# A hybrid attention layer on one Trainium2 core: the gated linear attention cut into pieces that stand between the units of the input projection

## The chip, the core and the metric

The kernel runs on one core of a Trainium2 chip. A core has five engines that run side by side and meet only at semaphores: TensorE (PE in the profile; its weight loads are listed as PEld), VectorE (DVE), ScalarE (ACT), GpSimd (POOL) and SyncE (SP), which here only issues DMAs. Work on data is done in SBUF, a memory of 128 partitions; TensorE writes to PSUM, eight banks of 128 partitions by 512 floats. The metric is the device time of one execution in microseconds (us); lower is better.

## What is computed

One layer over 1024 latent tokens and 256 context tokens of width 1024: a half-step SwiGLU FFN, then softmax attention and gated linear attention (GLA) from one input projection `w_in`, merged, and a second FFN. The part that the change touches, cut to its core:

```python
p_lat = split(n_lat @ w_in)      # q, k, v | gq, gk, gv, gz | low | gates   (also for the context)
attn  = block_attention(rope(norm(q)), rope(norm(k)), v)
# GLA, both directions, 4 heads, keys of 64, values of 128:
la = log_sigmoid(low @ w_decay + b_decay) / 16
b  = cumsum(la within a chunk)
o_inter = (gq * exp(b)) @ s                       # s: state at the chunk's edge
A[i, j] = sum_d gq[i,d] * gk[j,d] * exp(b[i,d] - b[j,d])      # j <= i
o = o_inter + A @ gv
s = exp(b_last) * s + (gk * exp(b_last - b)).T @ gv
gla = rms_norm(o) * g_gla * silu(gz)
y = sigmoid(gates_a + b_gate_a) * (attn @ w_branch[0]) + sigmoid(gates_b + b_gate_b) * (gla @ w_branch[1])
h = h + m_lat[5] * (y @ w_out)
```

## The kernel before, in words

Everything is kept with channels on the partitions and tokens along the free dimension. A weight block of 128 columns is a **panel**: SP loads it into `raw` (`load_panel`), DVE splits it into a high part `wh` and a low part `wl` (`split_panel`, L194 and L196), and TensorE multiplies in three passes, high by high, high by low, low by high (`three`, L219 to L221). Panels alternate between two slots; `panel_split` and `panel_used` count them.

The stage of the input projection (`win_*`) has 35 panels. A **unit** is one panel times one token chunk (512, 512 and, for nine of the panels, the 256 context tokens), 24 matmuls into one PSUM bank; the first two panels are done as a pair (6 units) while the norm of the FFN's result is still arriving, the other 73 units one after the other. Units go round all eight banks (`WIN_BANKS`), so TensorE may be eight units ahead of ACT, which evacuates each (`win_act`): k, v, gk, gv, low, q and gq stay in SBUF, gz (after Silu) and the sixteen gate panels (after Sigmoid with their bias) go through the four buffers `staged` to `gate_dram`.

Only when all units are done comes the GLA, in four steps written one behind the other on each engine:

- `gla_state_*`: values turned (L1225), decay logits (L1232), their log-sigmoid on ACT (L1267 to L1273, three table switches), 40 scans on DVE (L1306), decayed keys (L1315), then for 18 chunk steps the keys turned (L1240), copied by ACT (L1284), multiplied with the values (L1254) and added to the state by DVE (L1338, L1340).
- `gla_intra_*`: for each half of the latent tokens eight score levels. POOL forms the differences of `cum` (L1428 to L1431), ACT exponentiates them (L1405), DVE multiplies them into `qc` and `kc` (L1463, L1465), TensorE forms the scores (L1373), DVE takes the part that a mask selects (L1482). After eight levels TensorE applies scores to values and queries to states (L1385, L1388).
- `gla_out_*`: squares (ACT L1512), their sums (PE L1530), Ln and Exp (ACT L1519, L1523), then scaling, gating and the split into `glah` and `glal` on DVE (L1537 to L1544).
- `qk_*`: squares of k and q (ACT L1579), their sums (PE L1609), root, reciprocal, rotary embedding, and after that the softmax attention `att_*` and the merge.

Of the kernel before, what the change touches and what calls it, by code (L numbers as in the profile page):

```python
# [100 lines left out]
def build(nc, x, c, ctx_in, c_ctx, w_mod, b_mod, g_norm, w_ffn_up, w_ffn_down, w_in, g_q, g_k,  # L101
# [64 lines left out]
    part_loaded, gate0_loaded, select_loaded = rows_loaded[0:4], rows_loaded[4:8], rows_loaded[8]  # L166
    cols_ready = sem("cols_ready")
# [31 lines left out]
    def pn(p):  # L199
        return (p // 2, p % 2)  # L200
# [774 lines left out]
    gk_f, gv_f = at("gk_f", 0, [2, TOK]), at("gv_f", 10, [4, TOK])  # L975
    k_f, v_f = at("k_f", 30, [TOK]), at("v_f", 35, [TOK])
    q_f = at("q_f", 120, [4, SEQ])
    gq_f, low_f = at("gq_f", 193, [2, SEQ]), at("low_f", 201, [TOK])
    staged = at("staged", 164, [4, 512])

    la = at("la", 40, [4, TOK])
    kk = la
    cum = at("cum", 60, [4, TOK])
    vtok = at("vtok", 80, [N_CHUNKS, GLA_HEADS * DV])
    states = at("states", 100, [2, 9, 2, DV])
    wdec = at("wdec", 148, [512])
    ktok = at("ktok", 150, [2, 256])
    last = at("last", 152, [4, N_CHUNKS])
    elast = at("elast", 152.5, [4, N_CHUNKS])
    dexp = at("dexp", 154, [2, TOK])  # L990
    gla_o = at("gla_o", 10, [GLA_HEADS, SEQ])
    eq, ek = at("eq", 140, [2, 512]), at("ek", 144, [2, 512])
    qc, kc = at("qc", 148, [2, 512]), at("kc", 152, [2, 512])
    eqs, eks = [eq, at("eq_b", 48, [2, 512])], [ek, at("ek_b", 52, [2, 512])]
    qcs, kcs = [qc, at("qc_b", 164, [2, 512])], [kc, at("kc_b", 168, [2, 512])]
    scores = at("scores", 156, [2, 4, 2, P])
    qdec = at("qdec", 40, [2, 2, 512])
    gz_s = at("gz_s", 80, [GLA_HEADS, SEQ])
    gla_r = at("gla_r", 140, [8, 512])
    gla_n = at("gla_n", 201, [2, 512])  # L1000
    glah, glal = at("glah", 40, [GLA_HEADS, SEQ], F32R), at("glal", 56, [GLA_HEADS, SEQ], F32R)

# [85 lines left out]
    def ffn0_last_dve(dve):  # L1090
# [7 lines left out]
        for q in range(24):  # L1098
# [5 lines left out]
            if q == 20:  # L1104
                split_panel(dve, pn(win_p0))
# [1130 lines left out]
```

## Time and profile before

| | us |
|---|---|
| median of 3 runs | 3028.68 (3025.79 to 3031.61) |
| the profiled execution | 3022.72, span 3020.9 |
| PE busy in it | 2803.9 (93%) |
| DVE, ACT, POOL busy | 1502.4, 556.7, 508.0 |
| mean granted clock of TensorE | 0.953 of full |

The page cuts the span in 40 slices of 75.5 us. Each digit is the busy share of a slice in tenths, and PEclk is the clock that was granted to TensorE, in tenths of full speed (2.4 GHz; 5 is 1.2 GHz). The lines of engines show where the kernel leaves its dense pattern: slices 19 to 24 of the line of PE and of the clock.

```profile
PE   8999999999999999999456869998999999999998
...
PEclk9999999999999999999666679999999999999999
```

### The profile page before, as it was taken

The page shows a single profiled execution, that of the slowest core. Times are in us where ns is not written, and L with a number is a line of the kernel's source. Part 1 is how long each engine was busy: PE and PEld are TensorE (multiplying, and loading weights), DVE is VectorE, ACT ScalarE, POOL GpSimd, SP SyncE. Part 2 cuts the span into 40 slices and gives each one's busy share as a digit, 9 for nine tenths or more (in the row PEclk, how much of TensorE's full clock was granted, in tenths as well). Part 3 has the DMA queues.
Part 4 walks back from the last instruction along what each step waited for, and adds up shares of the span by engine and source line. Part 5 has one row for each costly group of instructions (what it writes and reads, how often), then busy time and mean ns, then how long its engine had stood idle before and what let it go on. Part 6 is the DMA issues. An engine that isn't in the chain of part 4 may idle for free. (4 is left out here: it accounts for less than half of the span.)

```text
span 3020.9 us, 35198 instructions
## 1 busy us (share of the span) xinstructions
PE 2803.9 (93%) x14298; PEld 2292.2 (76%) x14298; DVE 1502.4 (50%) x2336; ACT 556.7 (18%) x1039; POOL 508.0 (17%) x400
## 2 busy tenths in 40 slices
PE   8999999999999999999456869998999999999998
PEld 3888888888888788887255647776777888888887
DVE  7544445444434611111776488885645444444444
ACT  4100000000000411112422447773011000000002
POOL 0065655554200000000063001211000000000001
PEclk9999999999999999999666679999999999999999
DMA  7112122222111211332000100002421111111111
GB/s 271 46 60 70 60 68 89 84 84 94 54 35 42 84 37 43 94 98 75 0 1 1 42 1 1 1 1 91 156 68 35 49 49 44 49 46 49 49 49 70
DMA packets 192127, 176.65 MB, mean 58 GB/s; under 512 B 6989, under 2 KB 148602, under 8 KB 191994
## 3 DMA queue, kind: packets, MB, share of 16 engines
q1 hardware_dynamic: 186016, 164.22, 17.1%
q10 hardware_dynamic: 5978, 10.56, 0.9%
q8 instruction: 95, 1.56, 0.2%
q14 instruction: 38, 0.31, 0.0%
HBM read 155.89 MB, written 18.87 MB: 58 GB/s over the span
## 5 line engine op out<-in xcount | busy, mean ns | idle before, releaser
L219 PE MATMUL psum<-nh,wh 128*128 128x512 f32 (+2 forms) x1688 | 612.9, 363 | 1.4 <-DVE wl L196 1.4
L220 PE MATMUL psum<-nl,wh 128*128 128x512 f32 (+2 forms) x1688 | 612.2, 363 | 0.0
L221 PE MATMUL psum<-nh,wl 128*128 128x512 f32 (+2 forms) x1688 | 611.8, 362 | 0.0
L194 DVE CAST wh<-raw 128x1024 fp32r<-128x1024 f32 x175 | 125.8, 719 | 695.0 <-PE psum L221 689.4
L219 PEld LDWEIGHTS psum<-nh,wh 128*128 128x128 f32 (+1 forms) x1688 | 316.7, 188 | 53.8 <-DVE wl L196 1.8
L221 PEld LDWEIGHTS psum<-nh,wl 128*128 128x128 f32 (+1 forms) x1688 | 316.5, 188 | 51.4
L220 PEld LDWEIGHTS psum<-nl,wh 128*128 128x128 f32 (+1 forms) x1688 | 316.7, 188 | 50.6
L844 DVE SCALAR_TENSOR_TENSOR h<-psum,gates,h 128x512 f32<-128x512 f32 (+1 forms) x400 | 270.8, 695 | 150.9 <-PE psum L221 149.1
L219 PE MATMUL psum<-hidh,wh 128*128 128x512 f32 (+1 forms) x880 | 329.2, 374 | 11.3 <-DVE hidl L828 7.6
L812 ACT ACTIVATE silu_a<-psum 128x512 f32<-128x512 f32 (+1 forms) x110 | 61.2, 556 | 1488.1 <-PE psum L221 1488.1
L220 PE MATMUL psum<-hidl,wh 128*128 128x512 f32 (+1 forms) x880 | 324.8, 369 | 0.0
L221 PE MATMUL psum<-hidh,wl 128*128 128x512 f32 (+1 forms) x880 | 324.1, 368 | 0.0
L219 PE MATMUL psum<-n1h,wh 128*128 128x512 f32 x704 | 274.3, 390 | 0.5 <-DVE wl L196 0.5
L221 PE MATMUL psum<-n1h,wl 128*128 128x512 f32 x704 | 273.9, 389 | 0.0
L220 PE MATMUL psum<-n1l,wh 128*128 128x512 f32 x704 | 273.9, 389 | 0.0
L196 DVE TENSOR_TENSOR wl<-raw,wh 128x1024 fp32r<-128x1024 f32 x175 | 226.7, 1295 | 6.1
L823 DVE TENSOR_TENSOR prod<-silu_a,psum 128x512 f32<-128x512 f32 (+1 forms) x110 | 69.7, 634 | 303.2 <-PE psum L221 300.4
L219 PEld LDWEIGHTS psum<-hidh,wh 128*128 128x128 f32 x880 | 165.8, 188 | 47.6 <-issue 13.7
L221 PEld LDWEIGHTS psum<-hidh,wl 128*128 128x128 f32 x880 | 165.6, 188 | 28.5
L220 PEld LDWEIGHTS psum<-hidl,wh 128*128 128x128 f32 x880 | 166.0, 189 | 26.9
L927 POOL TENSOR_TENSOR y_rows<-y_scaled,g_row 128x1024 f32<-128x1024 f32 x4 | 9.5, 2377 | 922.9 <-ACT y_scaled L921 922.9
L219 PEld LDWEIGHTS psum<-n1h,wh 128*128 128x128 f32 x704 | 132.2, 188 | 28.6 <-DVE wl L196 0.9
(251 smaller groups left out, 3866.7 us busy)
## 6 DMA issues: line engine op xcount, KB each, us to landing
raw<-in_w_ffn_up_dram SPq DMA_DIRECT2D x88, 512.0 KB, 3.9
mod_part<-in_w_mod_dram SPq DMA_DIRECT2D x96, 256.0 KB, 4.2
raw<-in_w_ffn_down_dram SPq DMA_DIRECT2D x44, 512.0 KB, 3.4
raw<-in_w_in_dram SPq DMA_DIRECT2D x34, 512.0 KB, 3.8
mod_raw<-in_w_mod_dram SPq DMA_DIRECT2D x12, 1024.0 KB, 13.7
gates_saved<-staged ACTq DMA_DIRECT2D x40, 256.0 KB, 2.0
merge_gate<-gates_saved SPq DMA_DIRECT2D x8, 1024.0 KB, 5.0
x_rows<-in_x_dram SPq DMA_DIRECT2D x8, 512.0 KB, 7.8
```

Source lines behind the costliest of these rows:

```text
L194: nc.vector.tensor_copy(wh[:, par, 0:n], raw[:, par, 0:n]).then_inc(panel_split, 1)
L196: nc.vector.tensor_tensor(wl[:, par, 0:n], raw[:, par, 0:n], wh[:, par, 0:n].bitcast(F32), ALU.subtract).then_inc(panel_split, 1)
L219: pe.matmul(o, hi_w, hi_x, start=first, stop=False)
L220: pe.matmul(o, hi_w, lo_x, start=False, stop=False)
L221: return pe.matmul(o, lo_w, hi_x, start=False, stop=last)
L812: nc.scalar.activation(silu_a[:, c, 0:w], ps[c][:, 0:w], ACT.Silu).then_inc(self.a_free, 1)
L823: nc.vector.tensor_tensor(prod[:, c % 2, 0:w], silu_a[:, c, 0:w], ps[3 + c][:, 0:w], ALU.mult).then_inc(self.b_free, 1)
L844: nc.vector.scalar_tensor_tensor(hk, down, gates[:, self.gate_i, k, s:s + 1], hk, ALU.mult, ALU.add).then_inc(self.down_free, 1)
L927: nc.gpsimd.tensor_tensor(y_rows[:, i, :], y_scaled[:, i, :], g_row[:, :], ALU.mult).then_inc(y_gained, 1)
```

## The change

The GLA is no longer a stage of its own. Each of its pieces is tied to the number of a unit (`LOGIT_UNITS`, `SCAN_UNITS`, `VTURN_UNITS`, `BATCH_UNITS`, `ITEM_UNITS`, `OUT_UNITS` and others), and `win_pe`, `win_act` and `win_dve` call `decay_*`, `state_*` and `intra_*` behind every unit:

- The panels are reordered: low, gk, k, v, gv, gq, gz, q, gates. k, v and q are copied to `kvq_dram` through `staged` and loaded back at the end (`weave_end_sp`); the gates are stored as they are, and the sigmoid is done in the merge, on ACT.
- The units behind the pair use two PSUM banks in turn (`RING_BANKS`) in place of eight; the other six serve the GLA.
- The state steps run in 12 batches of up to 4 chunks, one head pair and direction at a time, behind units 32 to 48. The intra part is 32 **items**, four groups (head pair times half of the tokens) of eight levels, each half as wide as a level before (128x512 in place of 128x1024). They stand behind units 49 to 73, five items to every four units, so seven units have two. Behind units 55, 62, 68 and 74 stands the output of a group, behind the next unit its sums of squares.
- A group's result is stored to `gla_dram` and the whole loaded back as `gla_n`; its high part is made by ACT, its low part by POOL, in `qk_act` and `gla_low_pool`; DVE did both.

```diff
-    WIN_BANKS = (4, 6, 7, 5, 0, 3, 1, 2)
+    PAIR_BANKS = (4, 6, 7, 5, 0, 3)
+    RING_BANKS = (1, 2)
...
     def win_pe(pe, panel0, norm):
...
-            if u >= 8:
-                pe.wait_ge(win_evac, u - 7)
+            if u >= PAIR_UNITS + 2:
+                pe.wait_ge(win_evac, u - 1)
             for k in range(KT):
                 mm = unit_k(u, k)
             done(u, mm)
+            decay_pe(pe, u)
+            state_pe(pe, u)
+            intra_pe(pe, u)
...
     def win_dve(dve, panel0):
-        for i, (_, width, _, _) in enumerate(win):
-            if i >= 2:
-                split_panel(dve, pn(panel0 + i), KT * width)
+        dve.wait_ge(h_saved, 16)
+        nc.vector.memset(wdec[0:2 * RANK, :], 0.0).then_inc(dec_zero, 1)
+        split_panel(dve, pn(panel0 + 2), KT * win[2][1])
+        for u in range(PAIR_UNITS, N_UNITS):
+            i, c = win_units[u]
+            if c == 0 and i + 1 < len(win):
+                split_panel(dve, pn(panel0 + i + 1), KT * win[i + 1][1])
+            decay_dve(dve, u)
+            state_dve(dve, u)
+            intra_dve(dve, u)
...
+    LOGIT_UNITS = [6, 7, 8, 9, 10, 11, 35, 36, 37, 38, 39, 40]
+    LN_UNITS, SCAN_UNITS = [8, 11, 37, 40], [10, 13, 39, 42]
+    BATCH_UNITS = [32, 33, 34, 35, 36, 37, 42, 43, 44, 45, 46, 47]
+    ITEM_UNITS = [49 + 4 * n // 5 for n in range(N_ITEMS)]
+    OUT_UNITS = [ITEM_UNITS[N_SCORES * g + N_SCORES - 1] + 1 for g in range(N_GROUPS)]
...
+    def intra_act(act, u):
...
+        if u - 1 in OUT_UNITS:
+            g = OUT_UNITS.index(u - 1)
...
+            for par in range(2):
+                act.wait_ge(o_ss, 2 * g + par + 1)
+                nc.scalar.activation(gla_r[par][:, :], ps[OUT_PAIR[par]][:, :], ACT.Ln, bias=eps, scale=1.0 / DV)\
+                    .then_inc(o_ln, 1)
+            for par in range(2):
+                act.wait_ge(o_ln, 2 * g + par + 1)
+                nc.scalar.activation(gla_r[par][:, :], gla_r[par][:, :], ACT.Exp, scale=-0.5).then_inc(o_rs, 1)
...
+    def weave_end_sp(sp):
+        sp.wait_ge(g_oz, N_GROUPS)
+        wait_saved(sp, len(staged_units))
+        sp.dma_start(k_f[:, :], kvq_dram[0]).then_inc(kvq_loaded, 16)
+        sp.dma_start(q_f[:, :, :], kvq_dram[2:6, :, 0:SEQ].rearrange("n p t -> p n t")).then_inc(kvq_loaded, 16)
+        sp.dma_start(v_f[:, :], kvq_dram[1]).then_inc(kvq_loaded, 16)
+        sp.dma_start(rope_t[:, :, :], rope.rearrange("a p t -> p a t")).then_inc(rope_loaded, 16)
+        sp.wait_ge(panel_used, merge_p0)
+        sp.wait_ge(g_stored, 32 + 16 * N_GROUPS)
+        sp.dma_start(gla_n[:, :, :], gla_dram).then_inc(gla_back, 16)
...
     def qk_act(act):
...
+        act.wait_ge(kvq_loaded, 80)
         for u in range(len(qk_units)):
             square(u)
+        act.wait_ge(gla_back, 48)
+        for hd in range(GLA_HEADS):
+            nc.scalar.activation(glah[:, hd, :], gla_n[:, hd, :], ACT.Copy).then_inc(o_hi, 1)
...
     def merge_act(act):
+        for n in range(KT):
+            act.wait_ge(gate_loaded[n % 2], 16 * (n // 2 + 2))
+            for b in range(2):
+                a = A_BGATE + KT * b + n
+                g = merge_gate[:, n % 2, b, :]
+                nc.scalar.activation(g, g, ACT.Sigmoid, bias=cols_a[:, a:a + 1]).then_inc(m_gate, 1)
...
-            dve.wait_ge(gate_loaded[n % 2], 16 * (n // 2 + 2))
+            dve.wait_ge(m_gate, 2 * n + 2)
```

How the rows stand on TensorE. Before, behind the last three matmuls of the last unit (`nh`, `nl` are the normed input, `wh`, `wl` the panel) comes the whole state step:

```order
L219 MATMUL psum<-nh_50,wh 128x512
L220 MATMUL psum<-nl_51,wh 128x512
L221 MATMUL psum<-nh_50,wl 128x512
L1225 MATMUL psum<-cst,gv_f 128x128 x40
L1232 MATMUL psum<-low_f,wdec 128x512 x2
L1232 MATMUL psum<-low_f,wdec 128x256
```

Now, around unit 56 (lines are one higher in the changed file: L220 to L222 is `three`), with the end of the output of group 0 (L1457, L1459) and item 8 (L1482, `gk_f`) ahead of it, and the sums of squares (L1467) and item 9 behind it:

```order
L1457 MATMUL psum<-scores,vlat_119 128x128
L1459 MATMUL psum<-qdec,states 128x128 x2
L1482 MATMUL psum<-eq_123,gk_f 128x128 x8
L220 MATMUL psum<-nh_50,wh 128x512
L221 MATMUL psum<-nl_51,wh 128x512
L222 MATMUL psum<-nh_50,wl 128x512
...
L1467 MATMUL psum<-cum,cst 128x512 x2
L1482 MATMUL psum<-eq_124,ek_126 128x128 x8
```

What was one run of GLA matmuls behind the last unit is now groups of 2 to 24 matmuls between units.

On ACT, the end of the GLA before (`sq` and `gla_r` belong to the norm of the outputs):

```order
L1405 ACTIVATE ek_b<-ek_b 128x1024
L1512 ACTIVATE sq<-gla_o 128x512 x2
L1519 ACT_TABLE_LOAD
L1519 ACTIVATE gla_r<-psum,cols_b 128x512
...
L1523 ACT_TABLE_LOAD
L1523 ACTIVATE gla_r<-gla_r 128x2048 x2
```

Now, behind unit 56, between the evacuation of that unit (L1202, and L1205, its store) and the exponentials of items 10 and 11 (L1518):

```order
L1202 ACTIVATE staged<-psum 128x512
L1205 DMA gates_saved<-staged 128x512
L1500 ACT_TABLE_LOAD
L1500 ACTIVATE gla_r_132<-psum,cols_b 128x512
L1500 ACTIVATE gla_r_133<-psum,cols_b 128x512
L1504 ACT_TABLE_LOAD
L1504 ACTIVATE gla_r_132<-gla_r_132 128x512
L1504 ACTIVATE gla_r_133<-gla_r_133 128x512
L1518 ACTIVATE eq_123<-eq_123 128x512
L1518 ACTIVATE ek_125<-ek_125 128x512
```

The norm of a group, with its two table loads, now stands ahead of the exponentials of the next items, once per group.

On SP, the end of the stage before, from the last panels of `w_in` to the first of the merge:

```order
L205 DMA raw<-in_w_in_dram 128x8x128 x26
L1202 DMA cst<-in_shape_consts_dram 128x1152
L1205 DMA wdec<-in_w_decay_dram 16x256
L1206 DMA wdec<-in_w_decay_dram 16x256
L1504 DMA gz_s<-gates_saved 128x4x1024
L1572 DMA rope_t<-in_rope_tables_dram 128x2x1024
L205 DMA raw<-in_w_branch_dram 128x8x128
```

and now:

```order
L206 DMA raw<-in_w_in_dram 128x8x128
L1619 DMA gla_saved<-gla_f 128x2x512
L1625 DMA k_f<-kvq_saved 128x1280
L1626 DMA q_f<-kvq_saved 128x4x1024
L1627 DMA v_f<-kvq_saved 128x1280
L1628 DMA rope_t<-in_rope_tables_dram 128x2x1024
L1631 DMA gla_n<-gla_saved 128x4096
L206 DMA raw<-in_w_branch_dram 128x8x128
```

Three loads (k, q, v) now stand at the point where the attention begins, and `gla_n` behind the rotary table.

## Rows read from the trace of the kernel before

**Rows 1.** Stretches: length, busy of PE, PEld, DVE, ACT, POOL, clock, DMA share, GB/s

```profile
1046.00:1425.20 379.20, 378.42 (x1749) 312.23 (x1748) 58.91 (x63) 47.67 (x75) 0.00 (x0) 1.00 0.24 71
1425.20:1512.00 86.80, 39.67 (x218) 21.15 (x218) 57.54 (x124) 37.52 (x54) 0.00 (x0) 0.67 0.01 4
1512.00:1602.00 90.00, 59.86 (x376) 49.95 (x374) 56.96 (x68) 16.68 (x18) 46.55 (x36) 0.60 0.00 1
1602.00:1684.00 82.00, 55.51 (x358) 46.35 (x356) 50.17 (x56) 16.26 (x17) 26.86 (x20) 0.65 0.02 5
```

**Rows 2.** Chain that ended last, in order of time: start, us, what

```profile
1702.07 18.09 PE psum L1609 x84
1724.79 6.33 PE psum L1631 x28
```

**Rows 3.** Timeline of PE in the linear attention: start, us from first to last end

```profile
1431.63 1.98 PE L1232 MATMUL psum<-low_f,wdec 32*128 32x512 f32 x4
...
1497.48 0.67 PE L1254 MATMUL psum<-vtok,ktok 128*64 128x128 f32 x8 [0.38 <-DVE states L1340]
1498.08 0.44 PE L1240 MATMUL psum<-cst,la 128*128 128x128 f32 x2
...
1575.23 0.79 PE L1385 MATMUL psum<-scores,vtok 128*128 128x128 f32 x2
...
1577.11 0.79 PE L1385 MATMUL psum<-scores,vtok 128*128 128x128 f32 x2
...
1616.82 2.06 PE L1373 MATMUL psum<-qc,kc 64*128 64x128 f32 x32 [2.52 <-DVE kc L1465]
1623.22 3.79 PE L1373 MATMUL psum<-qc_b,kc_b 64*128 64x128 f32 x32 [4.35 <-DVE kc_b L1465]
...
1651.62 0.49 PE L1385 MATMUL psum<-scores,vtok 128*128 128x128 f32 x2 [2.85 <-DVE scores L1482]
...
1652.83 0.80 PE L1385 MATMUL psum<-scores,vtok 128*128 128x128 f32 x2
...
1691.02 2.22 PE L1530 MATMUL psum<-sq,cst 128*128 128x512 f32 x4 [0.23 <-ACT sq L1512]
```

**Rows 4.** Lines of DVE: duration ns min/median/max, first and last start

```profile
L1306 DVE TENSOR_TENSOR_SCAN cum<-cst,la x40: 395/397/424, 1459.8 to 1476.7; 128x128 f32<-128x128 f32 x40
...
L1465 DVE TENSOR_TENSOR kc_b<-gk_f,ek_b x8: 1206/2054/2056, 1529.2 to 1645.5; 128x1024 f32<-128x1024 f32 x8
...
L1482 DVE COPY_PREDICATED scores<-cst,psum x56: 694/718/761, 1537.5 to 1650.9; 128x512 f32<-128x512 int32 x56
```

**Rows 5.** Timeline of ACT around a table switch

```profile
1449.01 0.47 ACT L1267 ACTIVATE la<-psum,cols_b 128x256 f32<-128x256 f32 x1 [0.39 <-PE psum L1232]
1449.50 1.28 ACT L1270 ACT_TABLE_LOAD   x1
1450.79 1.27 ACT L1270 ACTIVATE la<-la 128x1280 f32<-128x1280 f32 x1
```

**Rows 6.** Groups by line and shape: busy us, mean ns, idle before

```profile
L1512 ACT ACTIVATE sq<-gla_o 128x512 f32<-128x512 f32 x8 | 4.9, 620 | 40.6 <-DVE gla_o L1447 40.6
...
L1519 ACT ACTIVATE gla_r<-psum,cols_b 128x512 f32<-128x512 f32 x8 | 5.5, 685 | 2.0 <-PE psum L1530 1.8
```

**Rows 7.** DMA issues: out<-in, count, KB each, median us from issue to landing

```profile
gates_saved<-staged ACTq DMA_DIRECT2D x40, 256.0 KB, 2.0
merge_gate<-gates_saved SPq DMA_DIRECT2D x8, 1024.0 KB, 5.0
...
gz_s<-gates_saved SPq DMA_DIRECT2D x1, 2048.0 KB, 8.0
...
rope_t<-in_rope_tables_dram SPq DMA_DIRECT2D x1, 1024.0 KB, 10.1
```

**Rows 8.** A stretch of 4 us, columns as in rows 1

```profile
1576.00:1580.00 4.00, 4.00 (x14) 3.10 (x14) 0.00 (x0) 0.00 (x0) 2.32 (x3) 0.50 0.00 0
```

**Rows 9.** Timeline of DVE: its first instruction on a gate in the merge

```profile
2088.82 0.69 DVE L2043 TENSOR_TENSOR ma<-psum,merge_gate 128x512 f32<-128x512 f32 x1 [1.24 <-PE psum L221]
```

More of the change, by code:

```diff
@@ L976, in build @@
+    glah, glal = at("glah", 40, [GLA_HEADS, SEQ], F32R), at("glal", 56, [GLA_HEADS, SEQ], F32R)
+    gla_n = at("gla_n", 56, [GLA_HEADS, SEQ])
     k_f, v_f = at("k_f", 30, [TOK]), at("v_f", 35, [TOK])
     q_f = at("q_f", 120, [4, SEQ])
[L978 to L985, printed above, removed]
@@ L1048, in build, with wait_saved @@
+    def wait_saved(eng, n):
+        for b in range(4):
+            eng.wait_ge(saved[b], 16 * len(range(b, n, 4)))
     win_done, win_evac = sem("win_done"), sem("win_evac")
@@ L1269, in gla_state_act @@
             act.wait_ge(g_abs, 3 * (j + 1))
-            nc.scalar.activation(la[:, j, :], la[:, j, :], ACT.Exp, scale=-1.0).then_inc(g_exp, 1)
-        for j in range(4):
+            nc.scalar.activation(a, a, ACT.Exp, scale=-1.0).then_inc(g_exp, 1)
             act.wait_ge(g_exp, j + 1)
-            nc.scalar.activation(la[:, j, :], la[:, j, :], ACT.Ln, bias=1.0).then_inc(g_ln, 1)
-        act.wait_ge(g_last, 4)
-        nc.scalar.activation(elast[:, :, :], last[:, :, :], ACT.Exp, scale=1.0 / GATE_NORM).then_inc(g_elast, 1)
@@ L1276, in gla_state_act @@
[L1276 to L1288 removed]
+            nc.scalar.activation(a, a, ACT.Ln, bias=1.0).then_inc(g_ln, 1)
@@ new lines, in intra_pe @@
+        for n in range(N_ITEMS):
+            if ITEM_UNITS[n] != u:
+                continue
+            g, lv, t, tok = item(n)
+            pe.wait_ge(g_qk, 2 * n + 2)
+            if n >= 2:
+                pe.wait_ge(g_pred, 2 * (n - 1))
+            else:
+                pe.wait_ge(g_state, N_STATES)
+            for cc in range(4):
+                for par in range(2):
+                    r = slice(DK * par, DK * par + DK)
+                    here = slice(cc * P, (cc + 1) * P)
+                    w = gk_f[r, t, tok][:, here] if lv == 0 else eks[n % 2][r, here]
+                    mm = pe.matmul(ps[SCORE_BANKS[n % 2][par]][:, here], w, eqs[n % 2][r, here],
+                                   start=True, stop=True)
+            mm.then_inc(g_sc, 1)
@@ L1545, in gla_out_dve, with gla_low_pool @@
+    def gla_low_pool(pool):
+        for hd in range(GLA_HEADS):
+            pool.wait_ge(o_hi, hd + 1)
+            nc.gpsimd.tensor_tensor(glal[:, hd, :], gla_n[:, hd, :], glah[:, hd, :].bitcast(F32), ALU.subtract)\
                 .then_inc(o_lo, 1)
```

701 lines of the change are left out of this document (364 added, 337 removed).

## The prediction

> **What bounds the kernel now.** I read the page first: PE is busy in 93% of the span, and only slices 19 to 24 of its line fall below 9, together with the granted clock. Then I cut the span at the stage borders. [rows 1]: in the input projection PE is busy for 378.4 of 379.2 us at full clock, while DVE, ACT and POOL have 59, 48 and 0 us of work. In the linear attention (GLA) that follows, PE is busy for 155 of 259 us, and at a mean clock of 0.60 to 0.67, so for most of it at 1.2 GHz and not 2.4. The stage starts at 1425.20, and the first sum of the softmax attention's norm starts at 1702.07 [rows 2]. So 276.9 us are spent, with PE waiting for other engines or running slow, right behind a stage in which the other engines are nearly empty. DVE paces the intra part: between two score levels PE waits for `kc` for 2.5 to 4.4 us [rows 3].
>
> **Term 1, what leaves: -276.9 us**, the whole stretch.
>
> **Term 2, what PE gets between the units.** Each piece still costs PE its own time, now at full clock if the clock holds. The instructions are as many as before (an f32 matmul is two instructions in the trace). From [rows 3], starts read against starts:
> - 32 items of 16 instructions: at full clock 32 instructions take 2.06 us, so 1.03 each, 33.0.
> - 32 output groups (one L1385, two L1388, six instructions). At half clock one takes 1577.11 - 1575.23 = 1.88, so 0.94 is the floor; with the clock falling it took 1652.83 - 1651.62 = 1.21. I take 1.0: 32.
> - 18 chunk steps of L1254: 1498.08 - 1497.48 = 0.60, 10.8.
> - 76 transposes: a pair shows 0.44 with its drain, a stream of eight instructions 0.67, so between 0.08 and 0.22 each; I take 0.15, as most stand in groups of four and eight: 11.4.
> - 24 instructions of L1232: 1.98 for four of 512 columns, 16 x 0.50 + 8 x 0.25 = 10.
> - 16 of L1530: 2.22 / 4 = 0.55, 8.8.
>
> Together +106 (floor 98, ceiling 118).
>
> **Term 3, waits in the woven stage.** 73 units make 378.4 us [rows 1]; 7 of them are of half size, so a full unit is 378.4 / 69.5 = 5.44 us. What must fit under it:
> - The ring of two banks (in place of eight): unit u waits for the evacuation of u-2, so ACT has a whole unit of slack. The log-sigmoid puts two table loads and two activations of 1280 columns (2 x 1.28 + 2 x 1.27 = 5.1 us, [rows 5]) behind one unit, which fits; the ten scans of 0.40 [rows 4] with three wide DVE instructions around them exceed a unit, but their taker stands two units on. I put 0 on this part.
> - Items: DVE must take the last item (two L1482, 1.44 us), split a panel in every other unit, and form two products of half the old width, 0.6 us each alone and 1.03 while POOL works (half of 1206 and of 2054 ns, [rows 4]). Some 3.5 to 5.5 us under 5.44 + 1.03: no wait in units with one item; in the seven with two, I expect about 1 us each: 8.
> - Behind an output, ACT must do the norm before the next exponentials. With E the end of unit 56: evacuation and store to E+1.0, table to 2.3, two Ln of 0.69 [rows 6] to 3.7, table to 4.9, two Exp (as the squares, 0.62) to 6.2, exponentials of item 10 to 7.4, its products to 8.6 or 9.5. PE, with sums 2.2 and item 9 1.0, ends unit 57 at E+8.7. So 0 to 0.8 us here and about as much for item 11; three such places, 4.
>
> Together +12. Below 0 is excluded, since a wait can only add. The ceiling is what a level waits now, (2.5 + 4.4) / 2 [rows 3], at half width 1.7, on 28 items: 48.
>
> [rows 5] also shows that the engine goes on at once at both ends of a table load: the activation before ends at 1449.48, the load runs from 1449.50, the next starts at 1450.79. The Trainium skill (ScalarE: Activation LUTs, What ACT_TABLE_LOAD costs) counts about 2.66 us for every switch of sets, the load and a drain of 1.38. By that rule each of the three norms would come 2.8 us later, and the sum would be 8 us higher; the trace disagrees, and the sum goes by the trace.
>
> **Term 4, the clock.** The units keep PE dense, so I expect 2.4 GHz in nearly all of the stage. But the output groups are a doubt: in 1576 to 1580 PE is busy for all of 4.00 us, and the clock is 0.50 [rows 8], and it had stayed so since the output began. So a run of eight groups can by itself be too thin for full clock. Half clock on all four outputs would cost 32 x 0.88 = 28; on the items too, (3.79 - 2.06) / 2 each [rows 3], 28 more. Nearest in kind is the dense stage around them; I take +8 (0 to 35).
>
> The Trainium skill (TensorE: Matmul & The Clock Gate, Why this matters for your kernels) advises to keep TensorE busy to hold the fast clock and puts the fall down to idle gaps. By it alone this term would be 0, and the sum 8 us lower; the row of a busy engine at 0.50 does not agree with busy time as the whole condition.
>
> **Term 5, the end of the stage.** The last unit is evacuated (0.6), stored (2.0 to landing, [rows 7]), and only then are k, q and v loaded, 3328 KB, for all of which ACT waits before its first square. The nearest row: 2048 KB of gz and 1024 KB of the rotary table queued behind it landed within 10.1 us, so 3328 KB need 10.9. With the issues and the first square (0.62, [rows 6]) it is +14.5 (12 to 18). PE has nothing then, and the norm that follows runs slow, as it does now.
>
> **Term 6, behind it.** `gla_n` (2048 KB) and the rotary table follow the three loads, some 10 us, under the 18.1 us of L1609 [rows 2]. ACT casts 4 x 1024 columns (about 1.05 each, 4.2 us) between its last square and the root; it has some 1.5 us to spare there, so the root comes 2.7 later, and with it the reciprocal, the v split and L1631. DVE's old tail (`gla_n`, `glah`, `glal`) ran beside L1609, so its going gives nothing. In the merge 16 sigmoids stand on an idle ACT; gates take 5.0 us to land [rows 7], a table load and two activations make 3.4 more, and DVE's first use at 2088.82 waits for PE [rows 9], so 0 to 2, I take 1. Together +3.7.
>
> **The sum:** 3022.7 - 276.9 + 106 + 12 + 8 + 14.5 + 3.7 = 2890, against the profiled execution. The median of the runs is 6 us (0.2%) above that execution; I give **2892**.
>
> **Rivals.**
> - *The items are paced by POOL, ACT and DVE, not by PE* (the ceiling of term 3): +36, 2928. For it: the chain differences, exponential, product, score is in series, and DVE's products double in time under POOL. Against it: an item may use a whole unit of 5.44 us, and POOL starts on it an item early. Chance 0.15.
> - *Half clock at outputs and items:* 56 in place of 8, 2940. Chance 0.11.
> - *Shorter than forecast:* no waits, full clock throughout, transposes at their floor: 2862 to 2872. Chance 0.09.
> - *Slower than before:* the f32 matmuls between the units pull the clock of the whole stage down to what they had alone, 0.63. Then 378 + 106 us of column-bound work become 768, which is +284: 3176. The point from which it decides: 135 us of gain are gone when the mean clock of the stage is below 484 / 619 = 0.78. Against it: more than three quarters of the work are the dense units that have 1.00 now. Chance 0.03.
> - *It isn't woven after all:* the rows of the order show GLA matmuls between the units, so only waits could undo it. Within the first rival.
>
> The forecast, 2872 to 2915, has 0.62. The range 2862 to 2938 leaves out about 0.15. A measurement of this kernel tells about 0.2% (6 us) from no change. Faster 0.96, same 0.01, slower 0.03: all cases but one lie 85 us or more below.
>
> **What the profile after would show.** The stage from the first unit behind the pair to the last should last 485 to 520 us with PE busy over 95% and clock over 0.95; L1482 16 instructions in about 1.0 us; the L1457/L1459 run in 8 us, 15 if the clock falls; PE idle before L1482 released by DVE `ek`, about 12 us in all, most in units with two items and behind a norm; a gap of about 15 us ahead of the sums of the qk norm, released by ACT's squares, these by the DMA of q or v; the root some 3 us later after it. I am wrong if idle before L1482 exceeds 40 us, if the clock in the stage is under 0.9, or if the DMA gap is over 20 us.

## The result, and the profile after

| | before | after |
|---|---|---|
| median | 3028.19 (3025.79 to 3031.61) | 2880.62 (2879.48 to 2885.50) |
| profiled execution | 3022.72, span 3020.9 | 2880.92, span 2879.0 |
| PE busy in it | 2803.9 (93%) | 2753.7 (96%) |
| mean granted clock | 0.953 | 0.983 |

The ratio is 0.9515, 95% interval 0.9498 to 0.9531. Beside the last experiments the kernel after ran again, with a median of 2884.27 and a ratio of 0.9528 (0.9513 to 0.9542); so two series of the same kernel differ by 0.13%.

The lines of PE and of the clock over the span of the kernel after, in 40 slices of 72.0 us. Before, five slices in a row stood at 4, 5, 6, 8 and 6; of this hole two slices are left, at 7 and 5:

```profile
PE   8999999999999999999997599979999999999998
...
PEclk9999999999999999999997799999999999999999
```

The woven stage and the gap behind it, in the columns of [rows 1]: length, busy of PE, PEld, DVE, ACT, POOL, clock, DMA share, GB/s.

```profile
1047.35:1543.80 496.45, 492.60 (x2711) 393.17 (x2712) 235.74 (x360) 151.02 (x240) 84.44 (x112) 1.00 0.23 69
1543.80:1559.40 15.60, 1.44 (x7) 0.88 (x6) 0.00 (x0) 1.35 (x3) 0.00 (x0) 0.71 0.71 281
```

The same units had 59 us of DVE work beside them before; now they have 236, and PE is still busy 99% of the time at full clock. Between the units and the first sum of the attention's norm lay 276.9 us [rows 1, 2]; now it is 14.2.

The longest waits of PE in the kernel after (what waited, for what, us in total, times, longest):

```profile
PE psum L1863 <- DVE ptl L1965: 28.2, 63, 1.8
PE psum L1701 <- ACT qk_sq L1666: 14.2, 1, 14.2
...
PE psum L1482 <- DVE ek L1593: 3.7, 3, 1.9
```

L1482 is now the score item. It waits 3.7 us in all, where a level waited 2.5 to 4.4 us each time [rows 3]. The new 14.2 us are the wait for k, q and v. PE in the woven stage (start, us from first to last end, count, idle time and releaser): a single item with the first matmul of the unit behind it, and the first output group of a run.

```profile
1376.98 1.16 PE L1482 MATMUL psum<-eq,ek 64*128 64x128 f32 x16 [0.74 <-DVE ek L1593]
1378.08 0.50 PE L220 MATMUL psum<-nh,wh 128*128 128x512 f32 x1
...
1404.83 0.38 PE L1457 MATMUL psum<-scores,vlat 128*128 128x128 f32 x2
...
1405.78 0.49 PE L1457 MATMUL psum<-scores,vlat 128*128 128x128 f32 x2
...
1406.84 0.49 PE L1457 MATMUL psum<-scores,vlat 128*128 128x128 f32 x2
```

The item is 16 instructions, the next unit begins 1.10 us after it began. An output group takes 1405.78 - 1404.83 = 0.95 for the first and 1406.84 - 1405.78 = 1.06 for those that follow, at full clock; it took 1.88 in [rows 3].

### The profile page after: what moved, and what is told of

It reads as the page before. It is cut to its first block, busy times and chain, and to the rows that moved or that the text cites. A ratio compares the mean times of both kernels' runs of the same rounds, so it can differ in the third digit from the quotient of the medians.

```text
span 2879.0 us, 35437 instructions
## 1 busy us (share of the span) xinstructions
PE 2753.7 (96%) x14298; PEld 2248.8 (78%) x14298; DVE 1489.3 (52%) x2354; ACT 597.9 (21%) x1118; POOL 528.6 (18%) x460
## 4 chain that ended last, share of the span: by engine, by line
PE 86%; DVE 6%; ACT 5%; issue 2%; DMA 1%; ACTq 0%; SPq 0%; DVEq 0%
PE psum L220 25%; PE psum L221 25%; PE psum L222 25%; DVE ptl L1965 2%; PE psum L1863 1%; ACT pth L1922 1%; ACT prob L1912 1%; PE psum L313 1%; PE psum L1881 1%; PE psum L1482 1%; PE psum L1882 1%; PE psum L1459 1%; PE psum L1876 1%; PE psum L407 1%; PE psum L1701 1%
## 5 line engine op out<-in xcount | busy, mean ns | idle before, releaser
L220 PE MATMUL psum<-nh,wh 128*128 128x512 f32 (+2 forms) x1688 | 619.3, 367 | 1.4 <-DVE wl L197 1.4
L222 PE MATMUL psum<-nh,wl 128*128 128x512 f32 (+2 forms) x1688 | 612.2, 363 | 0.0
L195 DVE CAST wh<-raw 128x1024 fp32r<-128x1024 f32 (+1 forms) x175 | 126.2, 721 | 519.0 <-PE psum L222 513.7
L220 PEld LDWEIGHTS psum<-nh,wh 128*128 128x128 f32 (+1 forms) x1688 | 317.0, 188 | 60.8 <-issue 3.4
L222 PEld LDWEIGHTS psum<-nh,wl 128*128 128x128 f32 (+1 forms) x1688 | 316.7, 188 | 51.9
L220 PE MATMUL psum<-hidh,wh 128*128 128x512 f32 (+1 forms) x880 | 330.0, 375 | 10.7 <-DVE hidl L829 7.6
L222 PE MATMUL psum<-hidh,wl 128*128 128x512 f32 (+1 forms) x880 | 324.8, 369 | 0.0
L220 PE MATMUL psum<-n1h,wh 128*128 128x512 f32 x704 | 274.3, 390 | 0.5 <-DVE wl L197 0.5
L222 PE MATMUL psum<-n1h,wl 128*128 128x512 f32 x704 | 273.9, 389 | 0.0
L197 DVE TENSOR_TENSOR wl<-raw,wh 128x1024 fp32r<-128x1024 f32 (+1 forms) x175 | 224.3, 1282 | 6.0
L220 PEld LDWEIGHTS psum<-hidh,wh 128*128 128x128 f32 x880 | 166.4, 189 | 46.9 <-issue 13.7
L222 PEld LDWEIGHTS psum<-hidh,wl 128*128 128x128 f32 x880 | 166.0, 189 | 28.8
L386 POOL TENSOR_SCALAR mod_part<-mod_part,silu_c 128x512 f32<-128x512 f32 x84 | 139.0, 1655 | 97.5 <-DMA mod_part<-in_w_mod_dram 97.5
```

The lines of the kernel that those rows point to most:

```text
L195: nc.vector.tensor_copy(wh[:, par, 0:n], raw[:, par, 0:n]).then_inc(panel_split, 1)
L197: nc.vector.tensor_tensor(wl[:, par, 0:n], raw[:, par, 0:n], wh[:, par, 0:n].bitcast(F32), ALU.subtract).then_inc(panel_split, 1)
L220: pe.matmul(o, hi_w, hi_x, start=first, stop=False)
L222: return pe.matmul(o, lo_w, hi_x, start=False, stop=last)
L386: nc.gpsimd.tensor_scalar(raw_part, raw_part, silu_c[:, k, 0:1], None, ALU.mult)\
```

## The experiments

Medians are to be compared with 2880.62 for the kernel after; those of the norm one unit later, of the tail and of both also with 2884.27, which ran beside them. Profiled executions of one program begin the woven stage up to 5 us apart (its first decay matmul starts at 1053.0, and at 1057.9 when the kernel ran again), so differences of a few us are read inside a stage, from start to start.

### The weaving undone

```diff
-            decay_pe(pe, u)
-            state_pe(pe, u)
-            intra_pe(pe, u)
+        for u in range(PAIR_UNITS, N_UNITS):
+            decay_pe(pe, u)
+            state_pe(pe, u)
+            intra_pe(pe, u)
```

and the same on ACT and DVE; the loads of gz and the stores of groups follow the panels on SP.

> The weaving alone is undone: the kernel after with every piece of the linear attention behind the last unit of w_in, in the same order, forms, buffers and DRAM traffic. If the gain is the overlap (my reading), the 380 us of the units come back at full clock and the pieces cost what DVE, ACT and POOL need one after another, at 1.2 GHz for much of it: 220 to 290 us behind the units, so the time is 2990 to 3070, about that of the kernel before. Rival: the gain is in the new form of the pieces (half the width, fewer waits, no reloads), and stays for a third or more: below 2980.

Measured: 3092.67 (3085.46 to 3099.88), ratio 1.021 (1.015 to 1.027). So weaving is worth 212 us, more than the whole change: the new form of the pieces (half the width, an order of steps made for being spread) is about 64 us slower than the old stage when it stands alone. My range for the first theory ended at 3070, so even that was too kind to the form; the rival is out. Waits of PE in it, and a stretch of it in the columns above:

```profile
PE psum L1484 <- DVE ek L1595: 72.2, 19, 5.0
...
1620.00:1700.00 80.00, 53.30 (x272) 41.75 (x273) 34.49 (x50) 16.54 (x28) 24.21 (x36) 0.52 0.04 14
```

The same items that wait 3.7 us when a unit of 5.4 us stands between them wait 72.2 us in a row, and in the stretch shown the clock is 0.52.

### The ring of two banks alone, in the kernel before

```diff
-        return ps[WIN_BANKS[u % 8]][0:m, 0:w]
+        return ps[WIN_BANKS[u] if u < 6 else WIN_BANKS[6 + u % 2]][0:m, 0:w]
...
-                pe.wait_ge(win_evac, u - 7)
+                pe.wait_ge(win_evac, u - 1)
```

> The kernel before with one part of the change alone: units behind the pair go through a ring of two banks and wait for the evacuation of the unit before the last. ACT has a whole unit (5.4 us) for 0.6 us of evacuation: no change, within 3 us of 3028. Rival: each unit pays for the nearer wait, 0.1 us or more x 73, +7 us or more.

Measured: 3029.07, ratio 0.9996 (0.9985 to 1.0007). No change; six banks were free for the taking.

### The price of an item: its matmuls twice

```diff
-            for cc in range(4):
+            for cc in [c for _ in range(2) for c in range(4)]:
                 for par in range(2):
```

> The kernel after with the eight matmuls of every score item done twice (the same values written again). It takes the price of an item apart: 1.18 us between two units now. If all of it is the 16 instructions: 32 x 1.18 = +38 us. If it is 1.03 (the row of the kernel before) and 0.15 for the change between the units and the item: +33 us, 2914. If PE's own time is hidden in part by waits for the products: less than +30.

Measured: 2902.92, +22.3, below all but the last expectation, which is the one that holds, though not alone. From the first to the last item's matmul, in the kernel after and here (duration ns, first and last start):

```profile
L1482 PE MATMUL psum<-eq,ek x448: 272/272/511, 1303.4 to 1507.3; 64*128 64x128 f32 x150
```

```profile
L1482 PE MATMUL psum<-eq,ek x896: 272/272/373, 1305.3 to 1530.7; 64*128 64x128 f32 x180
```

203.9 us became 225.4, +21.5. PE waits for `ek` nowhere any more: the longer items give DVE the time that it lacked, so some 5 us of waits are hidden, and 32 items cost 27 us, 0.85 to 0.9 each (from the last matmul of a unit to the first of the next, both by their starts, 1.41 us with a single item became 2.30). Of the 1.18 us between two units that a single item takes, 0.9 are its instructions and some 0.3 the change there and back. The 1.03 of [rows 3] is half of 2.06 us from the first start to the last end, so it held 0.9 and half of the last matmul's 0.27.

### Does a long run of small matmuls lower the clock? The output groups three times

```diff
-            for par in range(2):
+            for par in [p for _ in range(3) for p in range(2)]:
                 r = slice(DK * par, DK * par + DK)
```

> The kernel after with each of the four runs of eight output groups computed three times over (the same values written again, so the output is the same), 25 us in a row of the small matmuls that were at 1.2 GHz in the kernel before. Theory A: the small matmuls keep 2.4 GHz as long as PE is busy with them; 16 more groups at 1.04 in four places, +66 us, 2947, clock 1.00 in the runs. Theory B: a run of them is too thin and lowers the clock by itself once it is long; the later groups cost 1.9, up to 4 x 16 x 1.9 = +122 us and more where the units behind the run still have 1.2 GHz (some 3 us each), up to 3015, clock 0.50 to 0.7 in the runs.

Measured: 2951.12, +70.5, for 64 groups 1.10 each. Theory A. The first run of output groups lasts from 1349.03 to 1374.4; 25 us of it:

```profile
1349.10:1374.10 25.00, 25.00 (x148) 19.30 (x148) 0.00 (x0) 0.60 (x1) 0.00 (x0) 1.00 0.03 12
```

The stream is the one that was at 0.50 for all of 4.00 us in the kernel before [rows 8], and for the 20 us behind that as well (the stretch ahead of those rows, and the one behind):

```profile
1571.00:1576.00 5.00, 2.37 (x9) 1.77 (x9) 3.11 (x5) 0.00 (x0) 2.39 (x3) 0.79 0.00 0
...
1580.00:1600.00 20.00, 20.00 (x66) 15.29 (x65) 0.00 (x0) 0.00 (x0) 0.00 (x0) 0.50 0.00 1
```

The instructions are the same, and the other engines are nearly idle in both. The difference that the traces show is what PE did before: there it came out of waits (2.37 of 5.00 us busy), here out of dense units. So the doubt of term 4 blamed the wrong thing: these matmuls did not lower the clock here, and did not bring it back there. That what came before decides is read from these two stretches; no run changed it alone.

### The waits behind a group norm: without table loads

```diff
-                nc.scalar.activation(gla_r[par][:, :], ps[OUT_PAIR[par]][:, :], ACT.Ln, bias=eps, scale=1.0 / DV)\
+                nc.scalar.activation(gla_r[par][:, :], ps[OUT_PAIR[par]][:, :], ACT.Copy)\
...
-                nc.scalar.activation(gla_r[par][:, :], gla_r[par][:, :], ACT.Exp, scale=-0.5).then_inc(o_rs, 1)
+                nc.scalar.activation(gla_r[par][:, :], gla_r[par][:, :], ACT.Copy).then_inc(o_rs, 1)
```

> The kernel after with the logarithm and the exponential of the group norm in the weave replaced by plain copies, so that its table loads go (the output is another). Theory: the 3.2 us ahead of the second item of unit 65 come of DVE's queue (norm, panel split and take stand ahead of the products) and of POOL's late start, and the total stays within 2 us. Rival: the two table loads set it; the wait goes, and with any drain beyond the load itself at each switch, 3 to 8 us of the total, 2873 to 2878.

Measured: 2875.80, -4.8. The rival holds. From first to last item 203.9 became 199.1 us:

```profile
L1482 PE MATMUL psum<-eq,ek x448: 272/272/373, 1304.1 to 1503.2; 64*128 64x128 f32 x150
```

```profile
PE psum L1482 <- DVE ek L1593: 1.0, 1, 1.0
```

How two table loads of 1.28 us reach PE is seen on ACT and DVE ahead of the pair of unit 65, first in the kernel after:

```profile
1420.88 1.28 ACT L1500 ACT_TABLE_LOAD   x1 [0.44 <-PE psum L1467]
1422.17 1.27 ACT L1500 ACTIVATE gla_r<-psum,cols_b 128x512 f32<-128x512 f32 x2
1423.46 1.28 ACT L1504 ACT_TABLE_LOAD   x1
...
1426.33 0.62 ACT L1518 ACTIVATE ek<-ek 128x512 f32<-128x512 f32 x1
```

```profile
1426.98 0.69 DVE L1591 SCALAR_TENSOR_TENSOR eq<-gq_f,eq 128x512 f32<-128x512 f32 x1 [2.94 <-ACT ek L1518]
...
1436.32 0.69 DVE L1593 TENSOR_TENSOR ek<-gk_f,ek 128x512 f32<-128x512 f32 x1
...
1437.52 0.69 DVE L1593 TENSOR_TENSOR ek<-gk_f,ek 128x512 f32<-128x512 f32 x1
```

and with copies:

```profile
1423.87 0.88 DVE L1591 SCALAR_TENSOR_TENSOR eq<-gq_f,eq 128x512 f32<-128x512 f32 x1 [0.20 <-ACT ek L1518]
...
1433.10 0.68 DVE L1593 TENSOR_TENSOR ek<-gk_f,ek 128x512 f32<-128x512 f32 x1
...
1434.45 0.68 DVE L1593 TENSOR_TENSOR ek<-gk_f,ek 128x512 f32<-128x512 f32 x1
```

The exponentials of the item behind the norm end at 1426.95; DVE, idle for 2.94 us until then, works from 1426.98 to 1438.21 without a pause (two products, the norm, a panel split, a take, four products). PE waits for the second of the last four, the first item of the pair, which ends at 1437.01; the other two end 1.2 us later. With the copies the row starts, measured against the item of unit 64 (1428.33 and 1427.82), 2.6 us sooner, the first item's products end at 1433.78, and PE comes to the pair at 1434.58 and does not wait. DVE's queue is where the delay is stored, as I thought, but ACT puts it there.

The wait itself is only part of what these loads cost. In the kernel after, PE behind it and the clock in the columns above:

```profile
1437.07 3.28 PE L1482 MATMUL psum<-eq,ek 64*128 64x128 f32 x32 [1.87 <-DVE ek L1593]
```

```profile
1438.00:1440.00 2.00, 2.00 (x22) 1.99 (x20) 1.58 (x3) 0.00 (x0) 1.36 (x3) 0.50 0.60 207
```

The pair took 3.28 us; it takes 2.06 with the copies. So behind an idle time of 1.87 us PE ran at half clock for some 3 us.

The first activation of the norm starts 1.29 us after the start of the load ahead of it, and the next load 0.02 us after the activations' end (1422.17 + 1.27): no drain is seen. The Trainium skill (ScalarE: Activation LUTs, What ACT_TABLE_LOAD costs) has 2.66 us for a switch; the trace has 1.28 here as it had in [rows 5], and the trace decides.

### Two orders that should have removed those waits

The panel split behind the take and the products of its unit:

```diff
-            if c == 0 and i + 1 < len(win):
+            late = u >= ITEM_UNITS[0]
+            if c == 0 and i + 1 < len(win) and not late:
                 split_panel(dve, pn(panel0 + i + 1), KT * win[i + 1][1])
             decay_dve(dve, u)
             state_dve(dve, u)
             intra_dve(dve, u)
+            if c == 0 and i + 1 < len(win) and late:
+                split_panel(dve, pn(panel0 + i + 1), KT * win[i + 1][1])
```

> The kernel after with DVE's panel split behind the take and the products of its unit, from the first item on. If DVE's queue makes the 5.7 us of waits ahead of L1482, they fall to 3 or less and the total by 2 to 4 us (2877 to 2879); unit 65 then waits for ACT's exponentials behind POOL, about 1.5 us in place of 3.2. Rival: they are set by POOL and ACT alone: no change. Third: the splits become late for the next panel and units wait, slower.

Measured: 2884.28 (2882.94 to 2885.62), +3.7. The waits did not fall. The longest now stands at the item of unit 58, for which the split was put behind the norm and ahead of the take:

```profile
PE psum L1485 <- DVE ek L1596: 4.5, 2, 3.4
```

PE there, and the stretch in the columns of [rows 1]:

```profile
1383.32 1.95 PE L1485 MATMUL psum<-eq,ek 64*128 64x128 f32 x16 [3.37 <-DVE ek L1596]
```

```profile
1383.00:1386.00 3.00, 2.68 (x18) 2.36 (x19) 0.95 (x3) 0.24 (x1) 0.64 (x2) 0.58 0.58 196
```

This wait costs twice: after 3.4 idle us the item runs at half clock, 1.95 us in place of 1.16. From first to last item it is 204.5 us, against 203.9, so the rest of the 3.7 us is not in this stretch, and two series of the kernel after differ by as much; the kernel is not shown to be slower.

The exponentials ahead of the norm on ACT, and DVE's part of the norm one unit later:

```diff
+    NORM_UNITS = [OUT_UNITS[g] + (3 if g < N_GROUPS - 1 else 2) for g in range(N_GROUPS)]
...
+        if u not in QDEC_UNITS:
+            intra_exp(act, u)
         if u - 1 in OUT_UNITS:
...
-        if u - 2 in OUT_UNITS:
-            g = OUT_UNITS.index(u - 2)
+        if u in NORM_UNITS:
+            g = NORM_UNITS.index(u)
```

> One edit to the kernel after: in the unit of a group norm ACT does the exponentials of the next item ahead of the norm (its two table loads and four activations), and DVE does its part of the norm a unit later. Theory now (after the run with copies in the norm, which took 4.8 us and left 1.0 of the 4.2 us of waits): the table loads hold up the exponentials, these DVE's queue, and behind it the second item of units 58 and 65. So waits ahead of L1482 of 1 us or less, 2876 to 2879. Rival: the norm only moves, and the exponentials of the item after it wait in its place: waits as now, 2880 to 2882.

Measured: 2882.53 (2880.64 to 2884.78), 1.7 below the kernel after beside it, within what two series differ by; first to last item 202.8 us. The rival: the waits are 4.3 us, more than the 3.7 of the kernel after, now at units 59 and 66. The 1.1 us between 202.8 and 203.9 are no gain in waits: here PE stays at full clock behind them (1.16 us for the item behind 2.35 idle us), where the kernel after had its pair at half clock. DVE there, from the product of unit 58 to that of unit 59:

```profile
1380.51 0.74 DVE L1607 SCALAR_TENSOR_TENSOR gla_f<-gla_f,cols_b,gla_r 128x512 f32<-128x512 f32 x1
...
1383.58 1.10 DVE L195 CAST wh<-raw 128x1024 fp32r<-128x1024 f32 x1
...
1386.16 1.36 DVE L1569 COPY_PREDICATED scores<-cst,psum 128x512 f32<-128x512 int32 x2
1387.42 1.27 DVE L1582 SCALAR_TENSOR_TENSOR qdec<-gq_f,qdec 128x512 f32<-128x512 f32 x2
```

Norm, split, take and decayed queries now meet in one unit, and with the two products behind them they fill 9.4 us without a pause. Both orders point to the same: in the two or three units behind an output DVE has as much work as PE gives it time for, and a reordering only picks the unit that waits.

### The gap behind the stage: an early load

`KVQ_SAVED` is the number of saves up to the last of k, v and q; the loads no longer wait for those of the gates.

```diff
         sp.wait_ge(g_oz, N_GROUPS)
-        wait_saved(sp, len(staged_units))
+        sp.wait_ge(o_ln, 2 * N_GROUPS)
+        wait_saved(sp, KVQ_SAVED)
         sp.dma_start(k_f[:, :], kvq_dram[0]).then_inc(kvq_loaded, 16)
...
+        wait_saved(sp, len(staged_units))
         sp.dma_start(rope_t[:, :, :], rope.rearrange("a p t -> p a t")).then_inc(rope_loaded, 16)
```

> One edit to the kernel after: the loads of k, q and v are issued as soon as the last linear-attention group is stored (1536 us) and the saves of k, v and q are in, not behind the last gate save; the rotary table and gla_n stay where they are. If the gap of 14.2 us ahead of the norm's sums is the DMA behind the last save (my reading), ACT's first square follows the last evacuation at about 1546, PE's idle time ahead of its first sum falls from 14.2 to 1 or 2 us, and the time falls by the difference less what gla_n makes late: gla_n lands some 10 to 17 us after 1550, ACT casts it before the root, and would wait for it up to 4 us. So -8 to -12.5 us, 2868 to 2873. Rival: the early load collides with the last units' traffic or the gla_n wait takes all of it: -3 or less, 2878 and more.

Measured: 2871.35 (2868.58 to 2873.98), -9.3, ratio 0.9486 (0.9470 to 0.9502). PE and ACT behind the last unit, in the kernel after and here:

```profile
1558.64 1.15 ACT L1666 ACTIVATE qk_sq<-k_f 128x512 f32<-128x512 f32 x2 [12.77 <-DMA v_f<-kvq_saved]
```

```profile
1548.47 17.16 PE L1705 MATMUL psum<-cst,qk_sq 128*128 128x2 f32 x84 [3.97 <-ACT qk_sq L1670]
```

```profile
1547.70 1.15 ACT L1670 ACTIVATE qk_sq<-k_f 128x512 f32<-128x512 f32 x2 [2.56 <-DMA v_f<-kvq_saved]
```

PE's idle time fell by 10.2, from 14.2 to 4.0 us, not to 1 or 2: the loads could start only at 1535.59, once the last group was stored, and v landed 10.9 us after its issue, 2.6 us too late.

### The casts and the split of v moved

On top of the early load: v turned and split ahead of the sums, the casts of `gla_n` behind the copies of four later norm units.

```diff
-        for hd in range(GLA_HEADS):
-            nc.scalar.activation(glah[:, hd, :], gla_n[:, hd, :], ACT.Copy).then_inc(o_hi, 1)
         act.wait_ge(k_ss, len(qk_units))
...
+            if 4 <= u < 4 + GLA_HEADS:
+                hd = u - 4
+                act.wait_ge(gla_back, 48)
+                nc.scalar.activation(glah[:, hd, :], gla_n[:, hd, :], ACT.Copy).then_inc(o_hi, 1)
```

> The early load of the run before, and two moves behind it: ACT casts gla_n one head at a time behind the copies of four later norm units, not ahead of the root; v is turned by PE and split by DVE ahead of the norm's sums, not between them and the spread. If the 3.9 us of casts and the 4 us of v splits stand on the path (my reading of the stretch 1574 to 1584), it is a further 3.3 and 2 us and any wait for gla_n: 2862 to 2866, and from the first sum to the first spread 18 to 20 us in place of 24.9. Rival: the tail is paced by DVE's rotations, whose end doesn't move with their start: same as the early load alone, 2868 to 2873.

Measured: 2872.49 (2870.70 to 2877.46), the same as the early load alone. That is the number of the rival, but not its way. From the first sum of the norm to the first **spread** (the matmuls L1723, before L1631, which bring the norm's factors to the channels) the time fell as expected, from 24.0 to 20.5 us. But from there to the first score of the attention it grew from 58.0 to 62.2. POOL and DVE in one of the units with a cast:

```profile
1608.67 2.48 POOL L1640 TENSOR_TENSOR glal<-gla_n,glah 128x1024 fp32r<-128x1024 f32 x1 [98.94 <-ACT glah L1697]
```

```profile
1605.51 0.69 DVE L1799 TENSOR_TENSOR rot<-rot,rot_b 128x512 f32<-128x512 f32 x1
...
1608.99 0.69 DVE L1795 TENSOR_TENSOR rot_b<-psum,rope_t 128x512 f32<-128x512 f32 x1
1609.78 1.93 DVE L1799 TENSOR_TENSOR rot<-rot,rot_b 128x512 f32<-128x512 f32 x1
```

A cast releases POOL's subtraction (1608.67 to 1611.15), and the same DVE instruction takes 1.93 us beside it and 0.69 alone: 1.24 us more in three of the four units with a cast and 0.89 in the fourth, 4.6 in all, on the engine that paces this stretch; the stretch grew by 4.2. The instruction ahead of it, L1795, ran wholly beside POOL too and took 0.69 as always; it reads one of its operands from PSUM, L1799 reads both from SBUF. At its other end the turning of v, now ahead of the sums, had to wait 3.3 us for v itself. The rival had DVE as the pace, but neither theory had named POOL. ACT had the idle time; what followed from its work was not free.

### The tail with both lessons

q is loaded behind the last output, k behind the last logarithm, v behind the last store; `gla_n` ahead of the rotary table; v is turned and split ahead of the sums; the casts stand between the squares, where DVE has nothing to do.

```diff
+        sp.wait_ge(g_oz, N_GROUPS)
+        wait_saved(sp, KVQ_SAVED)
+        sp.dma_start(q_f[:, :, :], kvq_dram[2:6, :, 0:SEQ].rearrange("n p t -> p n t")).then_inc(kvq_loaded, 16)
+        sp.wait_ge(o_ln, 2 * N_GROUPS)
+        sp.dma_start(k_f[:, :], kvq_dram[0]).then_inc(kvq_loaded, 16)
         gla_store(sp, N_GROUPS - 1)
...
             square(u)
+            if 5 <= u < 5 + GLA_HEADS:
+                hd = u - 5
+                act.wait_ge(gla_back, 48)
+                nc.scalar.activation(glah[:, hd, :], gla_n[:, hd, :], ACT.Copy).then_inc(o_hi, 1)
```

> The tail with all that the runs showed: q loaded as soon as the last output group is done, k after the last logarithm, v after the last store of a group, so that all three are in before the last unit ends; gla_n ahead of the rotary table; v turned and split ahead of the norm's sums; the casts of gla_n between the squares, where ACT has 1.08 us of idle time in each unit and DVE has nothing that POOL's subtraction could slow. Expected: PE idle 1 to 1.5 us behind the last unit, sums to first spread 20.5 us, spread to first score 58 as in the kernel after (62.2 with the casts among the rotations). That is 16 us less than after: 2864 to 2867. Rival: the casts or gla_n's landing stretch the squares: 2868 to 2872.

Measured: 2865.38 (2863.12 to 2868.16), ratio 0.9467 (0.9453 to 0.9481), 18.9 below the kernel after beside it and 15.2 below its first median. PE and ACT in it:

```profile
1550.52 1.28 PE L1707 MATMUL psum<-cst,v_f 128*128 128x128 f32 x10 [0.73 <-issue]
1551.64 2.29 PE L1712 MATMUL psum<-cst,qk_sq 128*128 128x2 f32 x20
1554.20 4.59 PE L1712 MATMUL psum<-cst,qk_sq 128*128 128x2 f32 x24 [0.27 <-ACT qk_sq L1670]
...
1571.99 4.13 PE L1729 MATMUL psum<-cst,k_r 128*128 128x128 f32 x20 [2.52 <-ACT k_r L1683]
...
1629.52 0.79 PE L1857 MATMUL psum<-kh,qs 128*128 128x512 f32 x1 [8.56 <-DVE qs L1768]
```

```profile
1559.14 1.06 ACT L1677 ACTIVATE glah<-gla_n 128x1024 fp32r<-128x1024 f32 x1 [3.09 <-DMA gla_n<-gla_saved]
```

PE is idle for 0.73 us behind the last unit, sums to spread is 20.4, spread to score 57.5. The rival is there in small: the first cast waits 3.09 us for `gla_n`, and PE 1.97 us behind it. From the last unit's evacuation to the first score it was 1641.95 - 1545.28 = 96.7 us in the kernel after, and is 1629.52 - 1549.83 = 79.7.

### Both, and the kernel after again

> Both edits of the two runs before it, since they lie in different stretches: the gains add, 2860 to 2864, if neither is covered by something else; 2864 to 2867 if the norm's move gives nothing.

Measured: 2867.01 (2863.25 to 2868.67), ratio 0.9474 (0.9461 to 0.9487): the norm's move adds nothing.

> The kernel after itself, on the chip of the three runs before it, to compare with: 2879 to 2885.

Measured: 2884.27 (2880.59 to 2885.64). The best kernel is therefore the one with the new tail, 2865.38, 5.3% below the kernel before and 0.5 to 0.7% below the kernel after.

## Why the prediction was right, and where its terms were off

The forecast was 2892 (2862 to 2938), and 2880.62 came out; the sum against the profiled execution was 2890, and it took 2880.92. The forecast way is the one that was measured: the GLA's own stage went, its matmuls came back between the units at their own price, and a new gap opened behind the last unit. By its own terms, from the two traces:

- **Term 1**, -276.9: as it stood; the stretch is gone, and the experiment that put the pieces back behind the units brought it back and more.
- **Term 2**, +106: it was 112. From the first unit behind the pair to the end of the last, before took 380.4 us (the 0.8 us ahead of the GLA's first matmul in it) and after 497.9, +117.5. Of this 110.6 lies between the starts of a unit's last matmul and of the next unit's first, some 5.7 of it waits and what followed from them; the units themselves are 7.7 longer, since one behind a piece begins with a matmul of 0.50 in place of 0.39 us. The single prices were close (items 1.18 with the change of kind against 1.03, output groups 1.06 against 1.0). What I left out is what a unit loses when it starts behind a piece, 0.14 us on average in 54 units. It stayed below the ceiling of 118.
- **Term 3**, +12: it was 5.7, of which 3.7 is the idle time in the list of waits, 1.3 the pair of unit 65 at half clock, and the rest small delays. The ring gave 0, as its own experiment shows. The units with two items, for which I had put 8, do not wait unless a norm is near. All of it stands in the two units behind a norm: 0.4 in unit 57 and 0.8 in 58, 3.3 in 64 and 65, 1.2 in 71. The reckoning with E was right for the first unit (0 to 0.8), but the larger part comes a unit later, through DVE's queue, which I had not followed that far, and two of these places (58 and 71) have one item, where I had expected no wait. The failing step is the 8 us for pairs as such.
- **Term 4**, +8: it was 0 for the reason given, and 1.7 for another. The clock is 1.00 over the stage, and a run of output groups three times as long kept it for 25 us. The reason for the doubt was a row of a busy engine at 0.50; what the traces show ahead of that row is waits. The term had no place for half clock behind a single wait: it came once, behind the 1.87 us of unit 65, and cost 1.3 us there (counted in term 3) and 0.4 in unit 66, which is 5.73 us long in place of 5.35 (counted in term 2).
- **Term 5**, +14.5: 14.2. Loads, landings (3.9, 8.6 and 9.7 us) and first square came as reckoned, though the chain was avoidable, as the last tail shows.
- **Term 6**, +3.7: 1.3. The spread comes 24.9 us after the first sum where it came after 22.7 [rows 2], +2.2 and not 2.7; from there to the first score it is 57.6 in place of 58.5; the merge cost 0 of its 1, since DVE's first gate instruction still waits for PE (0.79 us, by the releaser).
- Not foreseen, and not of the change: the stage began 2.6 us later in this execution. The kernel after begins it 5 us apart in its two traces.

Together -276.9 + 117.5 + 14.2 + 1.3 + 2.6 = -141.3, and the executions differ by -141.8. With the half clock left in terms 2 and 3, terms 3, 4 and 6 were too high by 6, 8 and 2 us and term 2 too low by 6. That the sum is only 9 us off (2890 and 2880.92) is so in part because these misses cancel.

Of the rivals: the pace of POOL, ACT and DVE (2928) shows only behind norms; as long as a unit of 5.4 us lies between items it is hidden, and 72.2 us of waits appear once it doesn't. Half clock at outputs and items (2940) is out but for the one pair. So is the fall of the whole stage's clock, and that was the only case that ended above the kernel before. The "shorter than forecast" case (2862 to 2872) had the clock right but not the change between pieces.

## What to carry to other kernels

Work that waits for other engines costs hardly more than its PE time once it stands between units that are long enough for the other engines to turn one piece around; here 5.4 us, with 3.5 to 5.5 us of DVE reckoned for an item, and the same pieces cost 212 us more in a row. When a stage becomes dense, look at its two ends next: loads that wait for the last save of everything rather than for their own data cost 10 us here, and a cast that looks free on its engine is dear if it starts another engine beside the one that sets the pace; here it was dear only for the DVE instruction with both operands in SBUF. Count what a moved instruction releases, not only where it runs.

## What the runs showed of the hardware

- **The clock depends on where a stretch comes from.** The same small f32 matmuls with PE busy throughout ran at 0.50 for 24.00 us after a stretch with waits, and at 1.00 for 25.00 us after dense units. The Trainium skill (TensorE: Matmul & The Clock Gate, Why this matters for your kernels) puts the loss down to idle gaps and asks to keep the engine busy; the second stretch agrees, the first shows that being busy with such matmuls did not restore it.
- **The 84 sums of two columns neither held the full clock nor restored it.** In the kernel with the new tail they are entered at 1.00, 0.73 us of idle time behind the last unit. The first 20 take 2.29 us; then PE waits 0.27 us, and the next 24 take 4.59 us, nearly all at 0.50. That is ahead of the wait of 1.97 us and not behind it. They stay at 0.50 with PE busy for 8.00 of 8.00 us.

```profile
1550.00:1554.00 4.00, 3.41 (x30) 3.35 (x30) 2.74 (x5) 2.47 (x5) 0.00 (x0) 1.00 0.80 266
1555.00:1558.00 3.00, 3.00 (x16) 3.00 (x16) 0.00 (x0) 0.63 (x1) 0.00 (x0) 0.50 0.73 296
1561.00:1569.00 8.00, 8.00 (x39) 8.00 (x39) 0.00 (x0) 6.03 (x8) 8.00 (x4) 0.50 0.30 123
```

- **A short wait in a dense stage can be followed by half clock, and need not be.** Behind 3.37 us an item took 1.95 in place of 1.16 us, and behind 1.87 us the pair of the kernel after took 3.28 in place of 2.06. But behind 1.90 us in the kernel with the early load, and behind 2.35 us with the norm one unit later, the clock stayed at 1.00. In these traces the length of the wait alone does not tell which; comparisons of stages by 1 or 2 us carry this chance.
- **POOL beside DVE** made a DVE instruction with both operands in SBUF take up to 1.93 us in place of 0.69, while POOL's own took 2.48 in place of 2.32 (9.29 us for four in the kernel after, with almost nothing but PSUM reads of DVE beside them). A DVE instruction of the same size that reads one operand from PSUM took 0.69 both ways.
- **A change of kind** between 512-column f32r matmuls and an f32 piece of 16 instructions costs some 0.3 us there and back (1.18 us between two units, 0.9 for each further 16 instructions).
